# The attention core of a two-layer encoder, unrolled with one more chunk in flight

## The chip, the cores and the metric

The kernel runs on one core of a Trainium2 chip. The metric is the device time of one execution in microseconds (us), as the median over several runs. The core's engines are TensorE (PE; its weight loads are listed as PEld), VectorE (DVE), ScalarE (ACT), GpSimd (POOL) and SyncE (SP, which issues DMAs). Each has its own instruction stream and runs it in order; the streams meet through semaphores alone.

## The reference, cut to what matters

A sequence of 16 meta tokens and 512 tokens, of width 1024, goes through two layers. Each is a half-step SwiGLU FFN, a token mixer and another half-step FFN, all normalised. The mixer of layer 0 is RWKV-7; that of layer 1, which the change concerns, is sliding-window attention with 16 query heads, 4 key/value heads of size 64, a learned sink per head and a relative-position bias. The 512 tokens form 8 chunks of 64; each chunk looks at the 16 meta tokens, the chunk before it and itself.

```python
lc = jnp.einsum('bcqgrd,bckgd->bgrcqk', qc, kb).astype(f32) * scale + bias
lc = jnp.where(valid[:, None, :], lc, NEG_INF)
pc = softmax_with_sink(lc, sink[:, :, None, None, None])
oc = jnp.einsum('bgrcqk,bckgd->bcqgrd', pc.astype(v.dtype), vb).reshape(B, S, G, R, Dh)
o = jnp.concatenate([om, oc], axis=1).reshape(B, L, D)
return o @ w_o + b_o
```

The outputs of the meta queries do not reach the result, so the kernel computes the 8 chunks alone.

## The kernel before

`attention(...)` makes three parts: `start` (projections to queries, keys and values, the bias table), `attend` (the core, lines 2191 to 2395) and `o` (the output projection, through the shared helper whose matmuls are at line 287). All operands of the core are float32, and a float32 matmul shows as two records in the trace.

For a chunk c (slot s = c % 2) the core does the following.

- GpSimd (function `pool`) copies the meta bias (L2238, step `bias`), the queries (L2241, `q`), and for either half of the heads the meta keys (L2250, `km0`, `km1`) and the window's keys (L2252, `kb0`, `kb1`) into slot s, and last the values (L2260, `v`). The bias copy of c waits for the copy `v` of c-1, and the copy `v` of c waits for the values matmuls of c-2 (step `o`), which read the same slot.
- TensorE, scores (L2276): 8 matmuls (16 records of 144 columns; 80 in chunk 0) into PSUM banks 0 to 2 in groups of 3, 3 and 2 pairs of heads (`l0` to `l2`). They wait for `kb1` of c and for DVE's reads of the same bank of c-1.
- DVE, scores (L2353): scale plus bias for each group, from PSUM to `prob`; then the row maximum (L2359), the maximum with the sinks (L2362), its negative (L2365), and the sink's argument (L2367, `ts`).
- ScalarE, exponentials: one for the sinks (L2321) and eight with row sums (L2323, step `p`).
- DVE, normalisation: the sum (L2371), its reciprocal (L2373) and the product over all probabilities (L2376, `p`). This is `softmax`, `normed` in the changed kernel.
- TensorE, turned probabilities: 8 transposes of the window's part (L2289, banks 3 and 4, `tb0`, `tb1`) and 8 of the meta part (L2298, banks 5 and 6, `tm0`, `tm1`).
- The copies of these to SBUF: `tb0` and `tm0` on ScalarE (L2329, L2332), `tb1` and `tm1` on DVE (L2381, L2384). `ptb` and `ptm`, which they write, have one buffer each.
- TensorE, values: 8 pairs of heads, each with a matmul over the window (L2309) and one over the meta tokens (L2310) into bank 7 (32 records, step `o`).
- ScalarE's high half of the result (L2337, `hi`) and DVE's rest (L2389, `lo`), both to `x16` as float16.

The helper `chunks` sets the order on every engine: chunk 0 and 1 are written out, chunks 2 to 7 run in a hardware loop (`Fori`) of two chunks a turn with offsets from a register. Within a step for chunk c, TensorE does scores(c), turned(c-1), values(c-1); DVE does the scores of c, the copies of c-1, the normalisation of c, the rest of c-1; ScalarE the copies of c-1, the exponentials of c, the high half of c-1. `Steps` counts the semaphores; with `lead=2` each starts two chunks ahead, so that waits on chunks -1 and -2 pass. `hold` increments a semaphore of its own between waits on GpSimd.

Of the kernel before, what the change touches and what calls it, by code (L numbers as in the profile page):

```python
# [26 lines left out]
P = 128  # L27
D = 1024
KT = D // P
META = 16  # L30
# [67 lines left out]
def build(nc, xT, vecs, consts, w_gu, w_down, w_rkv, w_l1, w_g1, w_w2, w_a2, w_g2, w_out, w_q, w_k, w_v, b_v,  # L98
          w_o, rel_table, rel_hot, flip_rows, out):
    with ExitStack() as ctx:  # L100
# [1850 lines left out]
        def attention(T, T_out, ffn_before, table_from):  # L1951
# [64 lines left out]
            def bands(e):  # L2016
# [3 lines left out]
                for s in range(2):  # L2020
                    e.dma_start(rev_band[s * CH:(s + 1) * CH],
                                shifted(8 * s * RELS + RELS - WIN, [[RELS, 8], [1, WIN]])).then_inc(s_bias, 16)
                    for ch in range(NCH):
# [16 lines left out]
                            lambda e, k: e.wait_ge(b_dve.sem, b_dve.count("lo", NCH - 1)), (2, 3))  # L2040
# [150 lines left out]
            a_pool = Steps(sem("attn_pool"), ["bias", "q", "km0", "kb0", "km1", "kb1", "v"], lead=2)  # L2191
            a_pe = Steps(sem("scores_pe"), ["l0", "l1", "l2"], lead=2)
            a_dve = Steps(sem("softmax_dve"), ["l0", "l1", "l2", "mx", "mxs", "nm", "ts", "den", "rd", "p"], lead=2)
            a_act = Steps(sem("softmax_act"), ["es", "p"], lead=2)
            b_pe = Steps(sem("values_pe"), ["tb0", "tb1", "tm0", "tm1", "o"], lead=2)
            b_dve = Steps(sem("values_dve"), ["tb1", "tm1", "lo"], lead=2)
            b_act = Steps(sem("values_act"), ["tb0", "tm0", "hi"], lead=2)
# [3 lines left out]
            def chunks(e, *parts):  # L2201


                scores, turned, softmax, values = parts
# [6 lines left out]
                scores(0, 0, CH)  # L2211
                softmax(0, 0, CH)
                step(1, 1)
# [3 lines left out]
                turned(NCH - 1, 1, WIN)  # L2217
                values(NCH - 1, 1, WIN)

            def nothing(*chunk):  # L2220
                pass

            def pool(e):
                a_pool.open(e)
# [6 lines left out]

                def a(c_, s, nb):
                    e.wait_ge(a_dve.sem, a_dve.count("l2", c_ - 2))
                    e.wait_ge(a_pool.sem, a_pool.count("v", c_ - 1))
                    hold(e)
                    e.tensor_copy(bias_t[:, s, :, 0:META],  # L2238
                                  b_meta[:, bass.ds(c_, 1)].rearrange("p o u n -> p (o u) n")).then_inc(
                                      a_pool.sem, a_pool.step("bias"))  # L2240
                    e.tensor_copy(qc[:, s], q_all[:, :, bass.ds(c_ * CH, CH)]).then_inc(a_pool.sem, a_pool.step("q"))  # L2241
                    if nb == CH:
                        band = slice(META, META + CH)
                    else:
                        band = bass.ds(c_ * CH + (META - CH), WIN)
                    for par in range(2):
                        rows = slice(par * HD, (par + 1) * HD)
                        e.wait_ge(a_pool.sem, a_pool.count("kb0" if par else "q", c_))
                        hold(e)
                        e.tensor_copy(kx[rows, 2 * s + par, :, 0:META], kd[rows, :, 0:META]).then_inc(  # L2250
                            a_pool.sem, a_pool.step(f"km{par}"))
                        e.tensor_copy(kx[rows, 2 * s + par, :, META:META + nb], kd[rows, :, band]).then_inc(  # L2252
                            a_pool.sem, a_pool.step(f"kb{par}"))
                    if nb == CH:
                        e.wait_ge(freed, v_at + 1)
                        e.wait_ge(s_vw, 48)
                    e.wait_ge(b_pe.sem, b_pe.count("o", c_ - 2))
                    e.wait_ge(a_pool.sem, a_pool.count("kb1", c_))
                    hold(e)
                    e.tensor_copy(vx[0:nb, s], v_win[0:nb, bass.ds(c_, 1)].rearrange(  # L2260
            "p o n -> p (o n)")).then_inc(a_pool.sem, a_pool.step("v"))
                chunks(e, a, nothing, nothing, nothing)

            def pe(e):
                a_pe.open(e)
                b_pe.open(e)
# [3 lines left out]
                def a(c_, s, nb):  # L2270
                    for z, (u0, u1) in enumerate(groups):
                        e.wait_ge(a_pool.sem, a_pool.count("kb1", c_))
                        e.wait_ge(a_dve.sem, a_dve.count(f"l{z}", c_ - 1))
# [7 lines left out]
                def b(c_, s, nb):  # L2281
                    for h2 in range(2):
                        if h2 == 0:
                            e.wait_ge(a_dve.sem, a_dve.count("p", c_))
                            e.wait_ge(b_act.sem, b_act.count("tb0", c_ - 1))
                        else:
                            e.wait_ge(b_dve.sem, b_dve.count("tb1", c_ - 1))
                        for u in range(4 * h2, 4 * h2 + 4):
                            last = e.transpose(psum[0:nb, 3 + h2, (u % 4) * P:(u % 4 + 1) * P],  # L2289
                                               prob[:, s, u, META:META + nb], c("ident"))  # L2290
                        last.then_inc(b_pe.sem, b_pe.step(f"tb{h2}"))
                    for h2 in range(2):
                        if h2 == 0:
                            e.wait_ge(b_act.sem, b_act.count("tm0", c_ - 1))
                        else:
                            e.wait_ge(b_dve.sem, b_dve.count("tm1", c_ - 1))
                        for u in range(4 * h2, 4 * h2 + 4):
                            last = e.transpose(psum[0:META, 5 + h2, (u % 4) * P:(u % 4 + 1) * P],  # L2298
                                               prob[:, s, u, 0:META], c("ident"))
                        last.then_inc(b_pe.sem, b_pe.step(f"tm{h2}"))  # L2300

                def values(c_, s, nb):
                    e.wait_ge(b_act.sem, b_act.count("tm0", c_))
                    e.wait_ge(b_dve.sem, b_dve.count("tm1", c_))
                    e.wait_ge(a_pool.sem, a_pool.count("v", c_))
                    for u in range(8):
                        g, par = u // 2, u % 2
                        o = psum[par * HD:(par + 1) * HD, 7, g * P:(g + 1) * P]
                        e.matmul(o, vx[0:nb, s, g * HD:(g + 1) * HD], ptb[0:nb, u], start=True, stop=False)  # L2309
                        last = e.matmul(o, v_meta[:, g * HD:(g + 1) * HD], ptm[:, u], start=False, stop=True)  # L2310
                    last.then_inc(b_pe.sem, b_pe.step("o"))
                chunks(e, a, b, nothing, values)

            def act(e):
                a_act.open(e)
                b_act.open(e)
                warm(e, ACT.Exp)

                def a(c_, s, nb):
                    e.wait_ge(a_dve.sem, a_dve.count("ts", c_))  # L2320
# [6 lines left out]
                def b(c_, s, nb):  # L2327
                    e.wait_ge(b_pe.sem, b_pe.count("tb0", c_))
                    e.activation(ptb[0:nb, 0:4], psum[0:nb, 3, :].rearrange("p (u n) -> p u n", n=P),  # L2329
                                 ACT.Copy).then_inc(b_act.sem, b_act.step("tb0"))  # L2330
                    e.wait_ge(b_pe.sem, b_pe.count("tm0", c_))
                    e.activation(ptm[:, 0:4], psum[0:META, 5, :].rearrange("p (u n) -> p u n", n=P),  # L2332
                                 ACT.Copy).then_inc(b_act.sem, b_act.step("tm0"))

                def values(c_, s, nb):
                    e.wait_ge(b_pe.sem, b_pe.count("o", c_))
                    e.activation(x16[:, 0, :, bass.ds(c_ * CH + META, CH)],  # L2337
                                 psum[:, 7, :].rearrange("p (k n) -> p k n", n=CH), ACT.Copy).then_inc(
                                     b_act.sem, b_act.step("hi"))
                chunks(e, nothing, b, a, values)  # L2340

            def dve(e):
                a_dve.open(e)
                b_dve.open(e)
                e.wait_ge(turn_dve.sem, turn_dve.count("read"))

                def a(c_, s, nb):
                    segs = [(0, NKEY, 0)] if nb == WIN else [(0, META, 0), (META, CH, META + CH)]
                    for z, (u0, u1) in enumerate(groups):
                        e.wait_ge(a_pe.sem, a_pe.count(f"l{z}", c_))  # L2350
                        e.wait_ge(a_pool.sem, a_pool.count("bias", c_))
# [6 lines left out]
                    e.wait_ge(a_dve.sem, a_dve.count("l2", c_))  # L2358
                    e.tensor_reduce(mx, prob[:, s, :, 0:META + nb], AX_X, ALU.max).then_inc(  # L2359
                        a_dve.sem, a_dve.step("mx"))  # L2360
                    e.wait_ge(a_dve.sem, a_dve.count("mx", c_))
# [261 lines left out]
```

## Time and profile before

| | us |
|---|---|
| median of three runs | 2396.33 |
| lowest, highest | 2395.67, 2398.77 |
| the profiled execution | 2393.34 |
| its span | 2391.4 |
| the attention core in it (first scores to the output projection) | 1838.97 to 1972.17 |

The profile is of one execution; the times in its rows count from the start of the span, which leaves out about 2 us of the execution. TensorE is busy for 2249.9 us of the span, DVE for 1114.1, ScalarE for 790.8 and GpSimd for 585.5. The granted TensorE clock is told as a share of its full 2.4 GHz; its mean over the span is 0.943. The first matmul records of the core are those of line 2276, and the first record of the part behind it is one of line 287.

### The profile page before, as it was taken

The numbers are of one execution on the slowest core, as the hardware profiler recorded it, in microseconds if no ns is written. First come the engines' busy times: TensorE is split into PE (matmuls) and PEld (weight loads), VectorE is DVE, ScalarE is ACT, GpSimd is POOL, SyncE is SP. The second block draws the span as 40 slices with busy tenths as digits, with TensorE's granted clock in tenths as the row PEclk, the third lists the DMA queues.
The fourth block names the chain that finished last, engine by engine and source line by source line (L and its number), as shares of the span: only waits on it lengthen the run. The fifth ranks groups of instructions, "written<-read, shape, count | busy, mean of one in ns | idle before, by whom it ended". The sixth has DMA issues, their size and how long they took to land.

```text
span 2391.4 us, 51187 instructions
## 1 busy us (share of the span) xinstructions
PE 2249.9 (94%) x22812; PEld 1912.7 (80%) x22812; DVE 1114.1 (47%) x1471; ACT 790.8 (33%) x1347; POOL 585.5 (24%) x676
## 2 busy tenths in 40 slices
PE   7999999789689998999999999999998889999997
PEld 6888887678589984778888888888887557888886
DVE  5434317785655544563342274333274336533423
ACT  4333314751233331353332153333132334433320
POOL 2111114486132210351111151110062104311103
PEclk9999999889699996899999999999998669999998
DMA  4333312220000010223233123233223002323311
GB/s 153 126 105 102 122 60 92 73 72 19 1 3 4 4 38 18 110 91 109 104 109 122 54 71 124 89 115 112 75 62 106 0 0 83 108 93 107 136 59 36
DMA packets 28949, 183.37 MB, mean 77 GB/s; under 512 B 3216, under 2 KB 8144, under 8 KB 9792
## 3 DMA queue, kind: packets, MB, share of 16 engines
q1 hardware_dynamic: 27888, 178.79, 21.4%
q8 instruction: 178, 2.92, 0.5%
q0 software_dynamic: 848, 1.37, 0.3%
q14 instruction: 35, 0.29, 0.0%
HBM read 174.31 MB, written 4.30 MB: 75 GB/s over the span
## 4 chain that ended last, share of the span: by engine, by line
PE 85%; DVE 8%; POOL 3%; ACT 2%; issue 1%; DMA 0%; SPq 0%; POOLq 0%; DVEq 0%; ACTq 0%
PE psum L287 67%; PE psum L1503 6%; POOL h L347 1%; PE psum L2310 1%; PE psum L2309 1%; PE psum L1494 1%; PE psum L311 1%; PE psum L1835 1%; PE psum L1527 1%; PE psum L362 1%; PE psum L2276 1%; PE psum L1837 1%; DVE arena L339 1%; POOL x L398 1%; PE psum L2110 1%
## 5 line engine op out<-in xcount | busy, mean ns | idle before, releaser
L287 PE MATMUL psum<-x,split 128*128 128x256 f16 (+2 forms) x5424 | 621.0, 277 | 9.8 <-POOL x L398 6.3
L287 PEld LDWEIGHTS psum<-x,split 128*128 128x128 f16 (+1 forms) x5424 | 532.7, 98 | 93.4 <-issue 10.5
L287 PE MATMUL psum<-x,split_more 128*128 128x256 f16 (+1 forms) x2688 | 310.5, 277 | 1.5 <-DVE x L2389 1.5
L695 POOL TENSOR_TENSOR arena<-arena 128x256 f16<-128x256 f32 (+1 forms) x176 | 120.1, 682 | 772.3 <-ACT arena L544 772.3
L287 PEld LDWEIGHTS psum<-x,split_more 128*128 128x128 f16 x2688 | 264.8, 99 | 41.3 <-issue 1.9
L287 PE MATMUL psum<-arena,split 128*128 128x256 f16 (+2 forms) x2448 | 279.2, 277 | 4.0 <-ACT arena L1209 4.0
L287 PE MATMUL psum<-x,arena 128*128 128x256 f16 (+1 forms) x2400 | 275.1, 276 | 0.7 <-POOL x L932 0.5
L287 PEld LDWEIGHTS psum<-arena,split 128*128 128x128 f16 (+1 forms) x2448 | 241.2, 99 | 40.5 <-ACT arena L1209 4.7
L262 DVE SCALAR_TENSOR_TENSOR split<-stage,split 128x2048 f16<-128x2048 f32 (+2 forms) x77 | 192.4, 2499 | 161.4 <-ACT split L256 161.4
L287 PEld LDWEIGHTS psum<-x,arena 128*128 128x128 f16 x2400 | 235.1, 98 | 35.4 <-POOL x L932 1.5
L622 DVE SCALAR_TENSOR_TENSOR arena<-psum,arena 128x256 f32<-128x256 f32 (+1 forms) x176 | 75.5, 429 | 320.8 <-ACT arena L538 316.2
L538 ACT ACTIVATE arena<-psum 128x256 f32<-128x256 f32 (+1 forms) x176 | 68.3, 388 | 384.2 <-PE psum L287 384.1
L256 ACT ACTIVATE split<-stage 128x2048 f16<-128x2048 f32 (+2 forms) x77 | 155.3, 2017 | 28.9 <-PE psum L287 27.4
L438 ACT ACTIVATE arena<-arena 128x272 f32<-128x272 f32 (+1 forms) x96 | 38.9, 418 | 360.3 <-DVE arena L425 338.3
L287 PE MATMUL psum<-arena,split_more 128*128 128x256 f16 (+3 forms) x1248 | 144.8, 278 | 11.8 <-POOL arena L961 11.8
L425 DVE TENSOR_SCALAR arena<-psum 128x272 f32<-128x272 f32 (+1 forms) x80 | 33.3, 427 | 249.9 <-PE psum L287 249.9
L287 PEld LDWEIGHTS psum<-arena,split_more 128*128 128x128 f16 (+1 forms) x1248 | 123.3, 99 | 31.2 <-issue 12.2
L449 POOL TENSOR_TENSOR arena<-arena 128x272 f32<-128x272 f32 (+1 forms) x84 | 65.4, 779 | 326.1 <-ACT arena L438 323.0
L544 ACT ACTIVATE arena<-arena 128x256 f16<-128x256 f32 (+1 forms) x176 | 74.0, 421 | 185.9 <-DVE arena L627 185.9
L262 DVE SCALAR_TENSOR_TENSOR split_more<-stage,split_more 128x2048 f16<-128x2048 f32 (+2 forms) x38 | 94.3, 2481 | 83.5 <-ACT split_more L256 83.5
L287 PE MATMUL psum<-arena 128*128 128x256 f16 (+1 forms) x1056 | 120.0, 275 | 0.0
L262 DVE SCALAR_TENSOR_TENSOR arena<-stage,arena 128x2048 f16<-128x2048 f32 (+1 forms) x33 | 84.2, 2550 | 71.0 <-ACT arena L256 71.0
(220 smaller groups left out, 2830.7 us busy)
## 6 DMA issues: line engine op xcount, KB each, us to landing
stage<-in_w_gu SPq DMA_DIRECT2D x88, 1024.0 KB, 4.9
stage<-in_w_down SPq DMA_DIRECT2D x32, 1408.0 KB, 6.1
stage<-in_w_rkv SPq DMA_DIRECT2D x12, 1024.0 KB, 4.9
stage<-in_w_out SPq DMA_DIRECT2D x4, 1024.0 KB, 4.8
stage<-in_w_q SPq DMA_DIRECT2D x4, 1024.0 KB, 4.8
stage<-in_w_o SPq DMA_DIRECT2D x4, 1024.0 KB, 5.7
h_spill<-h SPq DMA_DIRECT2D x1, 2112.0 KB, 8.9
h<-h_spill SPq DMA_DIRECT2D x1, 2112.0 KB, 9.4
```

The source lines that it names most:

```text
L256: act.activation(job.split[:, 0, 0:job.cols], stage[:, job.u, 0:job.cols], ACT.Copy, scale=W_SCALE).then_inc(w_hi, 1)
L262: dve.scalar_tensor_tensor(out=job.split[:, 1, 0:job.cols], in0=stage[:, job.u, 0:job.cols], scalar=W_SCALE, in1=job.split[:, 0, 0:job.col ...
L287: last = pe.matmul(o, wt(wp, k), xs(xp, k), start=(k == 0 and wp == 0 and xp == 0), stop=(k == tiles - 1 and wp == 1))
L311: last = e.matmul(psum[:, b0 + b, 0:m], to, rows[:, a:a + m], start=True, stop=True)
L425: ins = dve.tensor_scalar(mix_out[:, m, a:a + n], bank(i, z)[:, 0:n], 1.0 / W_SCALE, None, ALU.mult)
L438: act.activation(osq[:, q % 2, 0:n], mix_out[:, m, a:a + n], ACT.Square).then_inc(out_sq, 1)
L449: pool.tensor_tensor(ssum[:, a:a + n], ssum[:, a:a + n], osq[:, q % 2, 0:n], ALU.add).then_inc(out_add, 1)
L538: e.activation(gate_s[:, no % 2, 0:n], bank(i)[:, 0:n], ACT.Sigmoid, scale=1.0 / W_SCALE).then_inc(gate_act, 1)
L544: e.activation(hid[s][:, 0, m, 0:n], hid32[:, no % 2, 0:n], ACT.Copy).then_inc(hid_hi, 1)
L622: e.scalar_tensor_tensor(out=gate_x[:, no % 2, 0:n], in0=bank(i)[:, 0:n], scalar=1.0 / W_SCALE ** 2, in1=gate_s[:, no % 2, 0:n], op0=ALU.m ...
L695: e.tensor_tensor(hid[s][:, 1, m, 0:n], hid32[:, no % 2, 0:n], hid[s][:, 0, m, 0:n], ALU.subtract).then_inc(hid_lo, 1)
L1503: last = e.matmul(o[p0:p0 + HD, q], a[p0:p0 + HD, 4 * f + q, 0:CH], b[p0:p0 + HD, 4 * f + q, 0:CH], start=(z == 0), stop=(z == len(terms) ...
```

## The change

The hardware loop and the helper `chunks` are gone, and each engine has its order written out in Python for all 8 chunks, with constant offsets:

| engine | order within the iteration i |
|---|---|
| TensorE | scores(i+1), values(i-1), turned(i) |
| ScalarE | exponentials(i+1), high half(i-1), copies of turned(i) |
| DVE | normalisation(i), scores(i+1), rest(i-1), copies of turned(i) |
| GpSimd | copies of i, as before |

Chunk 0 has its scores and exponentials ahead of the loop, and chunk 7 its values, high half and rest behind it. The semaphores are split into one for each group of steps and start at zero; a wait on a chunk before the first is left out (`after`). Waits added: values(i) for DVE's rest(i-1); DVE's scores(i) for the transposes of i-2 (`tm1`); both engines' copies of i for the values of i-1; GpSimd's query copy of i for the scores of i-2 by TensorE's own semaphore. DVE's wait for the exponentials of the chunk before ahead of L2365 is gone, as is `hold` in the core. The output projection waits for the same event under its new name. The core of the diff:

```diff
-                def step(c_, s):
-                    scores(c_, s, WIN)
-                    turned(c_ - 1, 1 - s, CH if isinstance(c_, int) and c_ == 1 else WIN)
-                    softmax(c_, s, WIN)
-                    values(c_ - 1, 1 - s, CH if isinstance(c_, int) and c_ == 1 else WIN)
-                with e.Fori(0, NCH // 2 - 1) as i:
-                    step(i * 2 + 2, 0)
-                    step(i * 2 + 3, 1)
+            def after(e, steps, name, i):
+                if i >= 0:
+                    e.wait_ge(steps.sem, steps.count(name, i))
...
             def pool(e):
+                for i in range(NCH):
+                    s, nb = i % 2, keys(i)
+                    after(e, a_dve, "l2", i - 2)
+                    after(e, a_pool, "v", i - 1)
+                    e.tensor_copy(bias_t[:, s, :, 0:META], b_meta[:, i]).then_inc(a_pool.sem, a_pool.step("bias"))
+                    after(e, a_pe, "l2", i - 2)
+                    e.tensor_copy(qc[:, s], q_all[:, :, i * CH:(i + 1) * CH]).then_inc(a_pool.sem, a_pool.step("q"))
...
+                    after(e, o_pe, "o", i - 2)
+                    e.wait_ge(a_pool.sem, a_pool.count("kb1", i))
+                    e.tensor_copy(vx[0:nb, s], v_win[0:nb, i]).then_inc(a_pool.sem, a_pool.step("v"))
...
             def pe(e):
+                scores(0)
+                for i in range(NCH):
+                    if i + 1 < NCH:
+                        scores(i + 1)
+                    if i:
+                        values(i - 1)
+                    turned(i)
+                values(NCH - 1)
...
             def act(e):
+                exps(0)
+                for i in range(NCH):
+                    if i + 1 < NCH:
+                        exps(i + 1)
+                    if i:
+                        high(i - 1)
+                    turned(i)
+                high(NCH - 1)
...
             def dve(e):
+                scored(0)
+                for i in range(NCH):
+                    normed(i)
+                    if i + 1 < NCH:
+                        scored(i + 1)
+                    if i:
+                        rest(i - 1)
+                    turned(i)
+                rest(NCH - 1)
```

## Rows read from the trace of the kernel before

**Rows 1.** Windows of the core and behind it: stretch, length, busy by engine, PEclk, DMA.

```profile
1838.97:1972.17 133.20, 114.01 (x513) 76.09 (x514) 55.87 (x107) 41.70 (x161) 20.09 (x50) 0.68 0.02 7
1972.17:2391.40 419.23, 401.17 (x3592) 356.49 (x3592) 174.66 (x206) 131.47 (x198) 95.69 (x124) 0.98 0.25 89
```

**Rows 2.** Windows, scores start to scores start: first and last of five periods.

```profile
1863.48:1879.74 16.26, 13.94 (x66) 9.35 (x65) 7.17 (x13) 5.17 (x20) 2.81 (x7) 0.71 0.01 1
...
1927.56:1943.44 15.88, 13.81 (x65) 9.53 (x64) 7.17 (x13) 5.17 (x20) 2.81 (x7) 0.71 0.00 0
```

**Rows 3.** Windows between changes of the granted clock, the last figure but two.

```profile
1850.40:1867.40 17.00, 14.82 (x54) 8.86 (x52) 6.69 (x13) 4.58 (x19) 2.81 (x7) 0.50 0.00 0
1867.50:1874.20 6.70, 4.38 (x31) 2.76 (x30) 3.97 (x10) 4.58 (x19) 0.00 (x0) 1.00 0.01 2
1874.30:1884.40 10.10, 10.10 (x38) 7.12 (x39) 3.51 (x5) 0.60 (x1) 2.81 (x7) 0.50 0.00 0
...
1939.20:1949.30 10.10, 10.10 (x40) 7.70 (x40) 3.93 (x6) 1.20 (x2) 0.40 (x1) 0.50 0.00 0
...
1952.80:1962.90 10.10, 10.10 (x37) 5.58 (x38) 2.66 (x5) 2.15 (x8) 0.00 (x0) 0.50 0.00 0
1963.00:1969.80 6.80, 5.98 (x37) 3.19 (x34) 1.03 (x2) 0.59 (x1) 0.00 (x0) 1.00 0.01 2
```

**Rows 4.** Waits in the core: waiter, releaser, us in total, times, longest.

```profile
POOL arena L2260 <- PE psum L2310: 80.5, 6, 17.7
...
PE psum L2309 <- DVE arena L2384: 12.2, 6, 2.4
```

**Rows 5.** Order of time in one period: start, us, engine, line, operation.

```profile
1879.74 4.21 PE L2276 MATMUL psum<-arena 128*128 128x144 f32 x16
1880.15 0.40 POOL L2260 COPY arena<-arena 128x256 f32 x1 [12.84 <-PE psum L2310]
...
1882.96 0.61 POOL L2252 COPY arena<-arena 64x512 f32 x1
...
1886.48 0.21 ACT L2321 ACTIVATE arena<-arena 128x8 f32<-128x8 f32 x1 [0.27 <-DVE arena L2367]
...
1887.89 0.43 PE L2309 MATMUL psum<-arena 128*64 128x128 f32 x2 [1.87 <-DVE arena L2384]
...
1889.90 0.17 DVE L2371 TENSOR_TENSOR arena<-arena 128x8 f32<-128x8 f32 x1 [2.24 <-ACT arena L2323]
...
1890.34 1.36 DVE L2376 TENSOR_TENSOR arena<-arena 128x1152 f32<-128x1152 f32 x1
...
1895.30 3.60 PE L2276 MATMUL psum<-arena 128*128 128x144 f32 x16
```

**Rows 6.** Order of time, two turned blocks, of chunks 4 and 7.

```profile
1915.39 1.04 PE L2289 MATMUL psum<-cst,arena 128*128 128x128 f32 x8
...
1916.27 1.04 PE L2298 MATMUL psum<-cst,arena 128*16 128x128 f32 x8
...
1960.65 1.97 PE L2289 MATMUL psum<-cst,arena 128*128 128x128 f32 x8
```

**Rows 7.** Windows with values matmuls alone, of chunks 0 and 7.

```profile
1853.69:1863.48 9.79, 9.79 (x32) 4.50 (x33) 1.73 (x3) 2.14 (x12) 0.00 (x0) 0.50 0.00 0
...
1964.50:1969.80 5.30, 5.25 (x30) 2.83 (x30) 0.00 (x0) 0.00 (x0) 0.00 (x0) 1.00 0.01 3
```

**Rows 8.** Order of time at the start of the core.

```profile
1848.93 1.48 DVE L2353 SCALAR_TENSOR_TENSOR arena<-psum,arena 128x432 f32<-128x432 f32 x3
1849.07 1.06 PE L2289 MATMUL psum<-cst,arena 128*64 128x128 f32 x8 [2.50 <-DVE arena L2376]
...
1852.44 0.21 ACT L2321 ACTIVATE arena<-arena 128x8 f32<-128x8 f32 x1 [1.16 <-DVE arena L2367]
```

**Rows 9.** Order of time, GpSimd's first bias copy and DVE beside it.

```profile
1834.26 2.27 DVE L262 SCALAR_TENSOR_TENSOR split<-stage,split 128x2048 f16<-128x2048 f32 x1
1834.62 2.07 POOL L2238 COPY arena<-arena 128x128 f32<-128x128 f32 x1 [34.15 <-DVE arena L2170]
```

More of the change, by code:

```diff
@@ L2220, in nothing, with keys @@
-            def nothing(*chunk):
-                pass
+            def after(e, steps, name, i):
+                if i >= 0:
+                    e.wait_ge(steps.sem, steps.count(name, i))
+            def keys(i):
+                return CH if i == 0 else WIN
             def pool(e):
-                a_pool.open(e)
                 for par in range(2):
@@ L2253, in a @@
                             a_pool.sem, a_pool.step(f"kb{par}"))
-                    if nb == CH:
+                    if i == 0:
                         e.wait_ge(freed, v_at + 1)
                         e.wait_ge(s_vw, 48)
[L2257 to L2262, printed above, removed]
+                    after(e, o_pe, "o", i - 2)
@@ L2302, in values, with turned @@
[L2302 to L2305, printed above, removed]
+                def turned(i):
+                    s, nb = i % 2, keys(i)
+                    e.wait_ge(n_dve.sem, n_dve.count("p", i))
+                    for name, b0, rows, c0, n in (("tb", 3, nb, META, nb), ("tm", 5, META, 0, META)):
+                        for h2 in range(2):
+                            after(e, t_dve2 if h2 else t_act2, f"{name}{h2}", i - 1)
+                            for u in range(4 * h2, 4 * h2 + 4):
+                                last = e.transpose(psum[0:rows, b0 + h2, (u % 4) * P:(u % 4 + 1) * P],
+                                                   prob[:, s, u, c0:c0 + n], c("ident"))
+                            last.then_inc(t_pe2.sem, t_pe2.step(f"{name}{h2}"))
@@ L2306, in values @@
+                def values(i):
+                    s, nb = i % 2, keys(i)
+                    e.wait_ge(t_act2.sem, t_act2.count("tm0", i))
+                    e.wait_ge(t_dve2.sem, t_dve2.count("tm1", i))
+                    e.wait_ge(a_pool.sem, a_pool.count("v", i))
+                    after(e, o_dve2, "lo", i - 1)
                     for u in range(8):
                         g, par = u // 2, u % 2
-                        o = psum[par * HD:(par + 1) * HD, 7, g * P:(g + 1) * P]
-                        e.matmul(o, vx[0:nb, s, g * HD:(g + 1) * HD], ptb[0:nb, u], start=True, stop=False)
@@ L2310, in values @@
-                        last = e.matmul(o, v_meta[:, g * HD:(g + 1) * HD], ptm[:, u], start=False, stop=True)
-                    last.then_inc(b_pe.sem, b_pe.step("o"))
-                chunks(e, a, b, nothing, values)
+                        o_ = psum[par * HD:(par + 1) * HD, 7, g * P:(g + 1) * P]
+                        e.matmul(o_, vx[0:nb, s, g * HD:(g + 1) * HD], ptb[0:nb, u], start=True, stop=False)
+                        last = e.matmul(o_, v_meta[:, g * HD:(g + 1) * HD], ptm[:, u], start=False, stop=True)
@@ L2314, in act, with exps @@
+                    last.then_inc(o_pe.sem, o_pe.step("o"))
+                scores(0)
[6 more added lines that the diff above has]
+                values(NCH - 1)
             def act(e):
-                a_act.open(e)
-                b_act.open(e)
                 warm(e, ACT.Exp)
-                def a(c_, s, nb):
-                    e.wait_ge(a_dve.sem, a_dve.count("ts", c_))
+                def exps(i):
+                    s, nb = i % 2, keys(i)
+                    e.wait_ge(a_dve.sem, a_dve.count("ts", i))
@@ L2332, in b, with high @@
                     e.activation(ptm[:, 0:4], psum[0:META, 5, :].rearrange("p (u n) -> p u n", n=P),
[L2333 to L2337, printed above, removed]
+                                 ACT.Copy).then_inc(t_act2.sem, t_act2.step("tm0"))
+                def high(i):
+                    e.wait_ge(o_pe.sem, o_pe.count("o", i))
+                    e.activation(x16[:, 0, :, i * CH + META:(i + 1) * CH + META],
@@ L2342, in dve, with scored @@
+                high(NCH - 1)
             def dve(e):
-                a_dve.open(e)
-                b_dve.open(e)
                 e.wait_ge(turn_dve.sem, turn_dve.count("read"))
-                def a(c_, s, nb):
+                def scored(i):
+                    s, nb = i % 2, keys(i)
                     segs = [(0, NKEY, 0)] if nb == WIN else [(0, META, 0), (META, CH, META + CH)]
+                    e.wait_ge(a_pool.sem, a_pool.count("bias", i))
+                    after(e, t_pe2, "tm1", i - 2)
@@ L2375, in softmax, with turned @@
                     pr = prob[:, s, :, 0:META + nb]
                     e.tensor_tensor(pr, pr, rd.unsqueeze(2).to_broadcast([P, 8, META + nb]), ALU.mult).then_inc(
[L2377 to L2380 removed]
+                        n_dve.sem, n_dve.step("p"))
+                def turned(i):
+                    nb = keys(i)
+                    after(e, o_pe, "o", i - 1)
+                    e.wait_ge(t_pe2.sem, t_pe2.count("tb1", i))
```

132 lines of the change are left out of this document (46 added, 86 removed).

## The prediction, made before the result was known

> **What bounds the kernel now.** I read the windows first, then the waits, then the order of time. The attention core runs from 1838.97 to 1972.17 us: 133.2 us, with TensorE busy for 114.0 of them and a granted clock of 0.68 [rows 1]. Behind it lie 419.2 us in which TensorE is busy for 401 at 0.98. Nothing in the change touches that stretch, its weights have a stage of their own, and so what the core gains or loses should reach the end in full. Five loop periods from 1863.48 to 1943.44 take 79.96 us, 15.99 each [rows 2].
>
> A period holds three blocks of TensorE work, on scores, turned probabilities and values. In the period shown, scores start at 1879.74, values at 1887.89, the next scores at 1895.30 [rows 5]. Only one gap is worth having: values wait for copies that DVE makes behind the scores' reductions, 12.2 us in six waits [rows 4]. The rest is TensorE's own time, and that hangs on its clock. The windows show the two levels, 0.50 (1.2 GHz) and 1.00 (2.4 GHz), in long stretches [rows 3]. All values work of chunk 0 ran at 0.50 for 9.79 us with TensorE never idle [rows 7], and the clock did not rise until the scores behind it (1867.5 [rows 3]). It then stayed at 1.00 for 6.7 us, in which TensorE worked 4.4 us only: transposes, the gap, the start of the values. Then it fell within the values. So values do not raise the clock, scores and transposes do, and a good part of what they gain is spent on a gap.
>
> **The three blocks at either level.** Values: 9.8 us low [rows 7]; high, 30 records in 5.30 us at 1.00, so 32 in 5.65 [rows 7]. Scores: 16 records, 4.2 us low [rows 5]; no row shows them all at the high level, so I bound them by half of that, 2.1, and by no gain at all, 4.2, and take 2.1 for a fully high block, as transposes nearly halve: eight take 1.04 us high against 1.97 low, and 0.88 high from start to the next eight's start (1915.39 to 1916.27) [rows 6]. A turned block is two such halves: 1.8 us high, about 3.4 low (0.88 x 1.97 / 1.04, twice).
>
> **What the new order removes.** On TensorE it becomes scores(i+1), values(i-1), turned(i). The copies that values(i-1) wait for belong to a block turned a whole period before. So the gap of 12.2 us goes; its upper bound is all of it, its lower one nothing.
>
> **What is late next.** GpSimd copies values, queries and keys into two slots. Its copy of v(i+1) waits for values(i-1) to be done, and it must come before the keys of i+2. Today that wait is 80.5 us in total and free [rows 4], since scores and turned lie between. In the new order scores(i+2) follow values(i-1) with only turned(i) between. From the end of values at 1879.74 GpSimd starts at 1880.15 and ends its last key copy at 1883.57 (1882.96 + 0.61) [rows 5]; I add 0.25 us for TensorE to start, an estimate below the 0.41 of that first handover. That is 4.1; with constant addresses in place of registers the handovers may be shorter. I take 4.0, in a range of 3.6 to 4.2 as long as nothing blocks GpSimd. Turned(i) fills 1.8 to 3.4 us of it; the rest, 0.6 to 2.2 us, is a new gap, now ahead of the scores.
>
> One steady period is therefore scores + values + 4.0: 2.1 + 5.65 + 4.0 = 11.8 us all high, 4.2 + 9.8 + 4.0 = 18.0 all low, against 15.99.
>
> **Other edits.** DVE's and ScalarE's orders have a ring of their own: normed(i), scored(i+1), exponentials(i+1), normed(i+1). Exponentials take 3.42 us (1886.48 to 1889.90), normed 1.80 (1889.90 to the product's end at 1891.70) [rows 5], scored 3.5 with its three reads back to back (1848.93 to 1852.44 [rows 8]) and up to 1.2 more where low scores pace the reads. Together 8.7 us, at most 9.9, under the 11.8 of TensorE and GpSimd: no cost in the steady part, since those two hide it; uncovered, a period could not be shorter than these 8.7 to 9.9. ScalarE's copies of a turned block stand behind the next exponentials, a delay hidden by the period they now have. The added waits (values on DVE's rest of the chunk before, copies on the values before) name events a block or more old: zero, with DVE's rest of a chunk 0.7 us as the price if one were late. The unrolled streams issue the same instructions with fixed addresses. The loop's turn costs nothing that the five periods show, so I take zero, between 0.4 us gained and 0.4 us lost a period (the handover at 1879.74 again), 3 us in all either way. The final wait of the output projection names the same event. SP's queue is untouched.
>
> **The sum over the core.** Turned(0) starts at 1849.07 as today, nothing before it having changed order. Scores(2) follow it, and values(0) wait for ScalarE's copies, now behind exponentials(1): those start at 1852.44 [rows 8], take 3.42, and two copies follow of 0.6 each: values(0) at 1857.1, 18.1 us after the core's start (today 1853.69). From there: 8 values blocks v, five stretches of 4.0, five scores blocks s (3 to 7), two times turned-to-values at the tail T (chunks 6 and 7, no scores between to hide copies; 1960.65 to 1964.50 today, 3.9 [rows 6, 7]; 2.9 if high), and 2.0 from the last values (1964.5 + 5.7 = 1970.2) to the projection at 1972.17.
> All high: 18.1 + 45.2 + 20 + 10.5 + 5.8 + 2 = 101.6. All low: 18.1 + 78.4 + 20 + 21 + 7.8 + 2 = 147.3. Today 133.2: so from 31.6 gained to 14.1 lost, and the clock decides.
> Where it will be: today a high stretch (6.7 us long in six of eight, 3.3 in two) holds idle time ahead of the values, 2.3 us in the one from 1867.5 [rows 3]. If it opens at the end of the scores, as at 1867.5, it now falls straight on the values and covers most of a block. Today's values blocks average about 8.0 us (7.4 in the period shown, 9.8 in chunk 0, 5.7 in chunk 7); I take v = 7.1, that is 3.6 us of it high, and s = 3.1, halfway, as some high stretches will open in the turned block before, and T = 3.5. These are choices between rows, not readings. Sum: 18.1 + 56.8 + 20 + 15.5 + 7 + 2 = 119.4, a gain of 13.8.
>
> **A rule against this.** The transposes of chunk 7 (from 1960.65 [rows 6]) came after values at 0.50, and by 1963.0 the clock was 1.00 with no scores near [rows 3]: transposes raised it. The Trainium skill, TensorE: Matmul & The Clock Gate, Part 4: PE-mode transpose, says that the full clock does not engage for transposes, as they do not count as busy in the same way; that is rival F, and the trace disagrees with it here.
>
> **Rivals.** A, forecast: high for a good part of the values, 8 to 18 gained. Chance 0.48.
> B, high nearly throughout: without the gap ahead of the values the clock never falls, up to 31.6 gained; say 24, 2369 by this execution. For it: values(7) ran high from 1964.5 to 1969.8 behind turned and a short gap. Against it: seven of today's eight high stretches ended inside values. 0.19.
> C, GpSimd is stretched. Its copy of 128 elements at 1834.62 took 2.07 us, against 0.61 for one of 512 [rows 5], and ended at 1836.7, just after DVE's SBUF-only instruction of 2.27 us did (1836.5) [rows 9]. If DVE's product of normed(i+1), 1.36 us [rows 5], lands on the key copies, each of five stretches is 1.4 longer: 7 back, gain 7. Against it: when everything is high the product starts at about the copies' end, and later when low. 0.15. (The Trainium skill, SBUF — State Buffer, SBUF: two separate sides, has this as an exclusive lock of a port pair between GpSimd and DVE instructions with two SBUF inputs; the trace agrees at this one place.)
> D, the other side: the clock stays low. Values have 9.8 us in which to lose it, the new gap of 0.6 us or more stands right before the scores, and scores behind a gap may be too short to raise it, as those from 1943.44 [rows 2], through which the level stayed at 0.50 up to 1949.3 [rows 3]. Every period is then 18.0 against 15.99, up to 14.1 slower in sum. It decides once v averages above 8.1 with s at 4.2, where the sum reaches today's 133.2. 0.08.
> E, no net gain: v stays at 8.0 with s at 4.2, 7.2 and 5.5 us more than in the sum: 132, about 1 gained. 0.06.
> F, transposes open no high stretch: s stays at 4.2, five times 1.1 more, a gain of 8.3. 0.04.
>
> **Numbers.** The profiled execution takes 2393.34 us with a span of 2391.4; less 13.8 it is 2379.5. The median of the timed runs stands 3.0 us above it, at 2396.33, so the forecast for that median is 2382.6. A alone spans 2378 to 2388; with B and C down to 2368, with the milder part of D and E up to 2396. A measurement of this kernel can tell about 0.2%, 4.8 us, from no change. Faster: A, B, F and most of C, 0.83. Same: a little of C, E, part of D, 0.11. Slower: 0.06.
>
> **What would show it.** Right: gap before values (L2309 of before, DVE's copies as releaser) gone; scores now released by GpSimd's key copies, 4.0 us after the values' end; periods of 13 to 14.5 us; high stretches lying on the values. Wrong: periods near 18 at 0.50 (D); GpSimd copies of over 1 us (C); a gap released by ScalarE or DVE in mid-loop, which would mean that their ring is longer than 9.9.

## The result, and the profile after

The changed kernel takes 2369.39 us in the median of four runs (2368.07 to 2370.23) against 2396.85 for the kernel before: a ratio of 0.9884, interval 0.9867 to 0.9901, 27.5 us less. The forecast was 2382.6 in a range of 2368 to 2396. The time lies in the range, 13.2 us below the forecast and 1.4 above the range's lower end.

The profiled execution took 2368.07 us with a span of 2365.9, 25.5 less than before. The windows of the core and of what is behind it, in the columns of [rows 1]:

```profile
1833.28:1946.87 113.59, 103.28 (x513) 68.39 (x513) 56.50 (x108) 40.82 (x161) 20.38 (x50) 0.73 0.06 21
1946.87:2365.90 419.03, 400.98 (x3592) 356.46 (x3592) 174.57 (x206) 131.49 (x198) 95.83 (x124) 0.98 0.25 89
```

Behind the core nothing changed (419.23 against 419.03). The core is 19.6 us shorter. Of these, TensorE's busy time gives 10.7 (114.01 to 103.28) and its idle time 8.9 (19.19 to 10.31). TensorE's instructions are the same, so less busy time means the same matmuls at a higher clock (0.68 to 0.73 in the mean). Another 5.7 us of the span lie ahead of the core (1838.97 to 1833.28). Most of it is in TensorE's first waits (order of time, the kernel after):

```profile
1833.28 1.98 PE L2253 MATMUL psum<-arena 128*128 128x80 f32 x16 [0.71 <-DVE arena L2170]
1838.16 3.90 PE L2253 MATMUL psum<-arena 128*128 128x144 f32 x16 [2.89 <-DVE arena L2352]
```

The first scores stand 0.71 us behind the last window of the values' projection, against 5.09 before (the idle time in the bracket of the row `1838.97 7.59 PE L2276` of the kernel before). That is 4.4 us. The last 1.3 lie further ahead, in stretches with the same work, and have no cause that a run here shows. The 2.89 us ahead of scores(1) are new, since before scores(0) and (1) ran as one block. The bracket names VectorE, but TensorE's weight load waits for GpSimd's keys of chunk 1, and those stand behind a copy that waits for a DMA (waits):

```profile
POOL arena L2240 <- DMA arena<-arena: 8.5, 1, 8.5
...
PEld psum L2253 <- POOL arena L2233: 3.0, 1, 3.0
```

One period and a half in order of time, in the columns of [rows 5] and from several answers of that view:

```profile
1872.36 3.63 PE L2265 MATMUL psum<-cst,arena 128*128 128x128 f32 x16
1872.50 0.40 POOL L2240 COPY arena<-arena 128x256 f32<-128x256 f32 x1 [9.23 <-PE psum L2279]
1874.96 0.62 POOL L2233 COPY arena<-arena 64x512 f32<-64x512 f32 x1
1875.79 2.16 PE L2253 MATMUL psum<-arena 128*128 128x144 f32 x16
1877.89 0.43 PE L2278 MATMUL psum<-arena 128*64 128x128 f32 x2
1884.34 3.67 PE L2265 MATMUL psum<-cst,arena 128*128 128x128 f32 x16
1887.81 2.96 PE L2253 MATMUL psum<-arena 128*128 128x144 f32 x16
```

L2265 is the turned block (16 records, both kinds), L2253 the scores, L2278 the first of the values. No bracket stands behind a TensorE row: it is never idle here. The turned block of 3.4 us (from its start to that of the scores) ends 0.2 us after GpSimd's chain, which runs from 1872.50 to 1875.58. The period is 12.02 us (1875.79 to 1887.81), against 15.99 before [rows 2]. Windows of three periods, and of the clock's stretches in them (the granted clock is the last figure but two, as in [rows 3]):

```profile
1875.79:1887.81 12.02, 12.02 (x66) 8.03 (x65) 6.93 (x13) 4.94 (x20) 2.83 (x7) 0.78 0.00 0
1887.81:1899.88 12.07, 12.07 (x65) 8.49 (x65) 6.95 (x13) 4.96 (x20) 2.83 (x7) 0.79 0.01 1
1899.88:1911.95 12.07, 12.07 (x66) 8.08 (x65) 6.95 (x13) 5.09 (x21) 2.83 (x7) 0.78 0.00 0
...
1865.90:1872.30 6.40, 6.40 (x39) 3.57 (x37) 3.50 (x8) 2.73 (x14) 0.00 (x0) 1.00 0.00 0
1872.60:1875.70 3.10, 3.10 (x16) 2.44 (x16) 1.38 (x2) 1.95 (x5) 2.73 (x7) 0.50 0.00 0
1876.10:1882.40 6.30, 6.30 (x42) 4.09 (x40) 5.50 (x11) 0.56 (x4) 0.00 (x0) 1.00 0.00 0
1882.80:1889.40 6.60, 6.60 (x29) 5.01 (x28) 2.64 (x6) 3.98 (x16) 2.83 (x7) 0.50 0.00 0
```

In the steady periods a high stretch is as long as before, 6.3 to 6.7 us in such windows, but TensorE works in all of it where it worked 4.4 of 6.7 [rows 3]. It opens in the scores or at the end of the turned block and covers most of the values or all of them, then the clock falls. In the tail the two high stretches are only half as long, 3.1 and 2.8 us.

Not everything is shorter. Values(0) now wait for ScalarE, whose copies stand behind the exponentials of chunk 1:

```profile
1845.84 0.21 ACT L2297 ACTIVATE arena<-arena 128x8 f32<-128x8 f32 x1 [4.72 <-DVE arena L2352]
...
1849.13 0.57 ACT L2307 ACTIVATE arena<-psum 64x512 f32<-64x512 f32 x1
...
1850.23 0.69 PE L2278 MATMUL psum<-arena 64*64 64x128 f32 x2 [3.86 <-ACT arena L2310]
```

### The profile page after: what moved, and what is told of

Read it like the earlier page. It is cut to its first block, busy times and chain, and to the rows that moved or that the text cites. A ratio compares the mean times of both kernels' runs of the same rounds, so it can differ in the third digit from the quotient of the medians.

```text
span 2365.9 us, 50902 instructions
## 1 busy us (share of the span) xinstructions
PE 2236.7 (95%) x22812; PEld 1905.0 (81%) x22812; DVE 1112.4 (47%) x1471; ACT 789.7 (33%) x1347; POOL 584.2 (25%) x676
## 4 chain that ended last, share of the span: by engine, by line
PE 86%; DVE 8%; POOL 3%; ACT 2%; issue 1%; DMA 0%; SPq 0%; POOLq 0%; ACTq 0%; DVEq 0%
PE psum L287 67%; PE psum L1503 6%; POOL h L347 1%; PE psum L362 1%; PE psum L1494 1%; PE psum L311 1%; PE psum L2279 1%; PE psum L2278 1%; PE psum L1835 1%; PE psum L1527 1%; PE psum L2265 1%; POOL x L398 1%; PE psum L1837 1%; DVE arena L339 1%; PE psum L2110 1%
## 5 line engine op out<-in xcount | busy, mean ns | idle before, releaser
L287 PEld LDWEIGHTS psum<-x,split 128*128 128x128 f16 (+1 forms) x5424 | 531.6, 98 | 92.0 <-issue 10.2
```

What stands on the lines that cost most here:

```text
L287: last = pe.matmul(o, wt(wp, k), xs(xp, k), start=(k == 0 and wp == 0 and xp == 0), stop=(k == tiles - 1 and wp == 1))
```

## The experiments

Each run was timed in five rounds beside the kernel before; the ratio is to it. "Core" is the time in the trace from the first scores to the output projection (133.20 before, 113.59 after), "head" the idle time ahead of the first scores (5.09 and 0.71).

**The head alone, on the kernel before.**

```diff
...
             def dve(e):
+                a_dve.open(e)
+                b_dve.open(e)
                 start.vector(e)
...
```

and likewise on the other engines, the old places removed.

> The kernel before with one edit: every engine opens its semaphores of the core before its start part instead of behind it, so GpSimd's copies of chunk 0 need not wait until VectorE has issued the last split. My theory (head): the wait for that opening is what held the first scores 5.1 us behind the last values window, and the changed kernel shows 0.7; so 4 to 5 us faster than before, first scores within 1 us of the last values window, loop periods unchanged at 16 us. Rival (the head's gain comes with the new order or the constants): within 1 us of before.

Ratio 0.9971, interval 0.9962 to 0.9979. Head 0.66, core 132.04. GpSimd's first copy moved from 1834.62 [rows 9] to 1825.49, under the projection of the values:

```profile
1825.49 0.29 POOL L2237 COPY arena<-arena 128x128 f32<-128x128 f32 x1 [25.51 <-issue]
...
1834.07 1.98 PE L2273 MATMUL psum<-arena 128*128 128x80 f32 x16 [0.66 <-issue]
```

The theory of the head holds: 4.4 us of idle time are gone with this one edit. The edit moves the opening on every engine; that VectorE's was the one that counted is shown by the run with the late head below. Scores(0) also run at the high clock now, 1.98 us for 16 records instead of 3.7: in the kernel before the clock had fallen to 0.50 in the gap ahead of them, at 1836.6, and here it is 1.00 up to 1839.7. By the ratio the run is 7.0 us faster (5.0 to 9.1), where 4 to 5 were expected. The trace places 4.4 in the head and 1.2 in the core, and nothing here places the rest.

**Unrolled, in the old order.**

```diff
-                scores(0)
                 for i in range(NCH):
-                    if i + 1 < NCH:
-                        scores(i + 1)
+                    scores(i)
                     if i:
+                        turned(i - 1)
                         values(i - 1)
-                    turned(i)
```

with the orders of ScalarE and VectorE put back to match.

> The changed kernel (unrolled, split semaphores, nothing to open) with the order of before on all engines: scores(c), turned(c-1), values(c-1) and the rest to match. My theory: unrolling by itself gives the head (4.4 us) and perhaps 1 us through shorter handovers, so 5 to 6 us faster than before and 21 to 22 slower than the changed kernel, periods 15.5 to 16 us with a gap of about 2 us before values. Rival (the registers, branches and counted waits cost time in the loop): 10 us or more faster than before.

Ratio 0.9959, 0.9947 to 0.9971, which the head alone reaches within the intervals. That is 9.8 us (7.0 to 12.7), more than the 5 to 6 expected, and the timed runs alone don't exclude the rival's 10. The trace decides: head 0.70, core 132.06, a period of 15.53 of which 1.88 are idle, the gap before the values:

```profile
1833.87:1965.93 132.06, 113.48 (x513) 74.94 (x514) 57.48 (x108) 41.58 (x161) 20.23 (x50) 0.69 0.05 18
1871.95:1887.48 15.53, 13.65 (x65) 9.38 (x64) 7.14 (x13) 5.17 (x20) 2.81 (x7) 0.72 0.00 0
```

The run before this one has the loop, the registers and the early head, and its core is 132.04; so they cost nothing to speak of. What the core gained is the order's: 132.06 against 113.59.

**The new order with the old head.**

```diff
             def pool(e):
...
+                e.wait_ge(dve_here, 1)
                 for i in range(NCH):
...
             def dve(e):
+                e.sem_inc(dve_here, 1)
```

> The changed kernel with GpSimd's first copies made to wait until VectorE has issued its last split, as they did before: the new order without the early head. My theory: 4 to 5 us slower than the changed kernel, hence 22 to 23 faster than before. Rival (the head is later hidden behind the 3.9 us for which values(0) wait for ScalarE): under 1.5 us slower than the changed kernel.

Ratio 0.9912, 0.9899 to 0.9925; about 6.7 us slower than the changed kernel by the ratios, with some 5 us either way by their intervals. Head 4.77, core 113.30. The first copy was again the long one, beside VectorE's last split:

```profile
1836.83 2.57 POOL L2226 COPY arena<-arena 128x128 f32<-128x128 f32 x1 [33.57 <-DVEq L2331]
...
1841.37 3.99 PE L2255 MATMUL psum<-arena 128*128 128x80 f32 x17 [4.77 <-POOL arena L2235]
```

Here GpSimd waits for VectorE alone, and the head is back; so it was VectorE's count, added behind its start work. Head and order add up: 4.1 us of head, the core unchanged. (In this trace the work ahead of the head also ended 4.0 us later than in the changed kernel's, in unchanged work and with no cause shown.)

**ScalarE's first copies ahead of the exponentials of chunk 1.**

```diff
                 exps(0)
+                turned(0)
                 for i in range(NCH):
                     if i + 1 < NCH:
                         exps(i + 1)
                     if i:
                         high(i - 1)
-                    turned(i)
+                        turned(i)
```

> The changed kernel with ScalarE's two copies of turned chunk 0 ahead of the exponentials of chunk 1 instead of behind them; ScalarE is idle there for 4.7 us. Theory: values(0) start at the end of VectorE's copies, 3 us earlier, and fall into the high clock that TensorE still has, so 3 to 6 us faster than the changed kernel. Rival (something else is late in its place: the next exponentials, or the clock's stretches fall elsewhere): within 1 us.

Ratio 0.9871, 0.9856 to 0.9885; core 110.63, 3.0 less. The wait of 3.86 us is one of 0.73, at 1846.93. The intervals of this ratio and the changed kernel's overlap; the trace shows the step, and the timed runs can't tell it.

**A third slot for the values' copies.**

```diff
-                    after(e, o_pe, "o", i - 2)
+                    after(e, o_pe, "o", i - 3)
...
-                    e.tensor_copy(vx[0:nb, s], v_win[0:nb, i])
+                    e.tensor_copy(vx[i % 3][0:nb], v_win[0:nb, i])
```

> The changed kernel with three slots for GpSimd's copies of the values instead of two, so the copy of chunk i+1 waits for the values of i-2 and the key copies of i+2 are early. Theory 1 (TensorE sets the pace: it goes from turned(i) into scores(i+2) without a gap, as the low-clock turned block is as long as GpSimd's chain, both 3.4 us): within 1.5 us of the changed kernel. Rival (the chain of GpSimd is the bound, as I had forecast): 1 to 2 us a chunk faster, 5 to 10 in all.

Ratio 0.9893, 0.9878 to 0.9908; core 113.69 against 113.59, and 3.4 us from the values' end to the scores as before. GpSimd's chain is not the bound: with the copies early, the turned block alone fills that time.

**GpSimd's query copy twice, in chunks 3 to 7.**

> The changed kernel with GpSimd's query copy done twice in chunks 3 to 7, in the chain from the end of the values to the next scores: 0.7 to 0.8 us more a chunk. Theory 1 (chain and turned block end together, no slack): the scores wait that long, 3.5 to 4 us slower in all for five chunks, a little more or less as the clock's stretches move. Rival (there is slack in the chain): within 1 us.

Ratio 0.9914, 0.9900 to 0.9928, 7.2 us slower than the changed kernel by the ratios; by the trace the core is 117.60, 4.0 more, as expected. TensorE now waits for GpSimd ahead of each of the five scores blocks (waits):

```profile
PE psum L2257 <- POOL arena L2237: 1.6, 5, 0.5
```

From turned block to scores it is 3.93 us in each of the five, against 3.43 in the changed kernel: 0.50 of the 0.7 us added. So the chain had about 0.2 us of slack: making it shorter gains nothing, and making it longer costs nearly all that is added. The other 1.5 us lie in other blocks; TensorE's busy time grew by 2.4 in all (105.68 against 103.28), so the clock had a part in them.

**Three slots for values, two for turned probabilities, orders unchanged** (control, on the kernel with the early first copies).

> The kernel with the early first copies, with three slots for the values' copies and two for the turned probabilities, all orders unchanged: a control for the next run. Both theories: within 1.5 us of the kernel with the early first copies if TensorE sets the pace, 5 to 10 us faster if GpSimd's chain does.

Ratio 0.9876, 0.9860 to 0.9891, against 0.9871 with the early first copies alone: no gain.

**Transposes mixed into the values.**

```diff
                     if i:
-                        values(i - 1)
-                    turned(i)
+                        values(i - 1, {2: lambda: turned(i, "tb0"), 3: lambda: turned(i, "tb1"),
+                                       5: lambda: turned(i, "tm0"), 6: lambda: turned(i, "tm1")})
+                    else:
+                        turned(i)
```

(each number is a pair of heads, with the transposes that are issued ahead of it; on ScalarE and VectorE the copies of i come before the high half and rest of i-1).

> As the run before, but the four groups of transposes of chunk i stand between the values matmuls of chunk i-1 instead of behind them, on TensorE; ScalarE and VectorE copy them before the high half and the rest of i-1. Same instructions. Theory (a long run of values matmuls is what loses the high clock): fewer or no falls, periods from 12 down to 10 to 11 us, 6 to 14 us faster than its control, mean clock of the core above 0.80. Rival (the clock falls all the same, and the values of i now wait for the high half of i-1): within 2 us of the control or up to 8 slower.

Ratio 0.9905, 0.9890 to 0.9921, core 117.10: 7 us slower than its control, as the rival had it; the 6 to 14 us faster of the theory did not come. Yet the windows of its clock show both sides:

```profile
1853.60:1867.00 13.40, 13.40 (x50) 7.95 (x50) 6.22 (x12) 4.94 (x20) 2.97 (x6) 0.50 0.01 1
1867.40:1890.90 23.50, 22.74 (x144) 14.20 (x142) 15.21 (x28) 9.77 (x40) 7.10 (x15) 1.00 0.00 1
1891.40:1904.40 13.00, 13.00 (x49) 7.90 (x48) 5.97 (x12) 4.94 (x20) 3.17 (x6) 0.50 0.00 0
1904.90:1925.00 20.10, 18.20 (x113) 10.79 (x112) 11.71 (x24) 9.77 (x40) 0.55 (x2) 1.00 0.01 1
```

These high stretches are 23.5 and 20.1 us, three times those of the changed kernel (the longest in the kernel with the early first copies is 10.1, from 1841.6). That speaks for the theory that the long run of values had ended them, but does not show it alone, since ScalarE and VectorE changed their order as well. And the low ones are 13 us, some 10 of them mixture (1853.6 to scores at 1863.6, 1891.4 to scores at 1900.8): in it the clock stays at 0.50, and it rises 3.5 to 3.8 us into the scores behind it. The falls came beside short waits of TensorE, of 2.6 us for chunk 1's probabilities, 0.3 and 0.5 at 1888.2 and 1890.1, and 2.0 at the tail.

**The same with those waits worked on.** Chunk 1 unmixed; ScalarE's high half ahead of its copies; the last values in PSUM bank 0.

```diff
+                    if i == 1:
+                        values(0)
+                        turned(1)
-                    if i:
+                    elif i:
                         values(i - 1, {2: ...
```

> The kernel with the transposes mixed into the values, with its three stalls worked on: chunk 1 unmixed (its transposes waited 2.6 us for VectorE and the clock fell), ScalarE's high half ahead of the copies (values and transposes of chunk 4 and 5 waited 0.3 and 0.5 us and the clock fell again), and the last values into a free bank so as not to wait for VectorE's rest. Theory (a mixed stream keeps a high clock as long as nothing stalls it, and can't raise a low one): once high, all later periods near 10.2 us with no fall before the tail; 10 to 20 us faster than the mixed kernel, 2353 to 2363 us. Rival (the long high stretch was chance): still 2370 or more.

Ratio 0.9839, 0.9826 to 0.9853, core 103.49. One high stretch of 54 us, with periods of 10.2 us in it (scores at 1869.16, 1879.36, 1889.54, 1899.73):

```profile
1859.30:1913.70 54.40, 52.09 (x327) 32.26 (x325) 38.79 (x71) 24.89 (x102) 11.91 (x22) 1.00 0.00 1
1869.16:1879.36 10.20, 10.20 (x66) 6.44 (x65) 7.30 (x13) 4.85 (x21) 3.84 (x7) 1.00 0.01 2
1914.00:1940.90 26.90, 23.77 (x86) 11.84 (x85) 4.07 (x5) 6.77 (x8) 0.00 (x0) 0.50 0.00 1
```

It ended 2.1 us behind a wait of 1.6 us ahead of values(6). That the waits alone ended the stretches is not shown: chunk 1 changed its order as well, and this stretch went on through waits of 0.50 us at 1860.9 and 0.18 at 1862.6, about as long as the two beside the fall at 1891.0 in the first mixed kernel. It was not chance: the next two versions of this kernel have the same stretch, 54 us (plain tail) and 51 us (values copied later).

**The last values into a free bank, alone** (on the kernel with the early first copies).

> The kernel with the early first copies, and the last values into a PSUM bank that is free by then: values(7) no longer wait for VectorE's rest of chunk 6, but for their own copies only. Theory: the gap ahead of the last values is set by the copies of their own transposes as much as by the rest, so within 1 us of the kernel with the early first copies. Rival: 1 us or more faster.

Ratio 0.9870, 0.9855 to 0.9885, against 0.9871: nothing, as expected; the wait ahead of values(7) stays 0.8 us.

**A plain tail: chunk 7's transposes behind the values of chunk 6.**

```diff
-                    if i == 1:
-                        values(0)
-                        turned(1)
+                    if i in (1, NCH - 1):
+                        values(i - 1)
+                        turned(i)
```

> The tuned mixed kernel with the transposes of chunk 7 behind the values of chunk 6 instead of among them. In the mixed tail the clock fell at the stall ahead of values(6) and then stayed low for the mixture and all of the last values (24.0 us from values(6) to the end of values(7); the unmixed tail of the kernel with the early first copies took 22.2). Theory: a low mixture can't raise the clock, a dense turned block may: 1 to 4 us faster. Rival (values at the low clock take their 9.8 us in either order): within 1 us.

Ratio 0.9826, 0.9813 to 0.9840, median 2354.66 us: the lowest of the study, 43 us under the kernel before timed beside it. The interval overlaps that of the run before, but the core's 3.6 us less are what was expected. Its core is

```profile
1833.66:1933.57 99.91, 91.10 (x512) 58.35 (x513) 57.28 (x108) 39.87 (x161) 23.37 (x50) 0.87 0.07 24
1911.58:1932.10 20.52, 19.67 (x80) 10.34 (x80) 3.36 (x5) 1.78 (x3) 0.00 (x0) 0.64 0.00 1
```

and the tail, in the second row, 20.5 us instead of 24.0.

**Values copied behind the next chunk's keys.** GpSimd's copy of values(0) waits for a DMA, and scores(1) wait behind it.

> As the run before, and GpSimd copies the values of a chunk behind the keys of the next one, so the scores of chunk 1 no longer stand 2.9 us behind those of chunk 0 for a copy that waits for a DMA. Theory: scores(1) move up by 2.9 us, but turned(0) stays bound by the chain over VectorE and ScalarE, so 0 to 1 us faster. Rival (scores(0) and (1) back to back change where the clock's first stretches fall): 2 us or more either way.

Ratio 0.9835, 0.9819 to 0.9850: not faster, and the timed runs can't tell it from the run before. Scores(0) and (1) ran as one block of 4.67 us, but turned(0) then came 4.5 us later. The clock fell by the end of that gap: the turned block took 3.55 us instead of 1.94, and the core 101.92 instead of 99.91.

## Why the prediction was right, and where it was off

The sum's terms as they were put, and as the trace of the kernel after has them, block start to block start:

| term | forecast | measured |
|---|---|---|
| core's start to values(0) | 18.1 | 16.95 |
| 8 values blocks | 8 x 7.1 = 56.8 | 8 x 7.04 = 56.3 |
| 5 stretches, values' end to scores | 5 x 4.0 = 20 | 5 x 3.43 = 17.2 |
| 5 scores blocks | 5 x 3.1 = 15.5 | 5 x 2.59 = 12.9 |
| 2 turned-to-values at the tail | 7.0 | 8.7 |
| last values to the projection | 2.0 | 1.5 |
| core | 119.4 | 113.6 |

- **"Turned(0) starts at 1849.07 as today, nothing before it having changed order"** failed, and it is the step that cost most: turned(0) started at 1842.47. The order had not changed, but the diff let all semaphores start at zero, and with that took away VectorE's opening count, which stood behind its whole start part. The prediction has no term for this; it was put at nothing without a reason, though the change was listed. The run with the early opening and the one with the late head each put 4.1 to 4.4 us on it. In the sum it would have made 2378.2.
- **The gap before the values** went as forecast, in the middle of the core. Ahead of chunk 0 the wait for ScalarE is what the sum had in it (forecast 1857.1 less 1838.97; measured 1850.23 less 1833.28); the run with the first copies ahead shows that the order of one pair of copies avoids it.
- **GpSimd's chain** was mis-sized. I took 4.0 us in a range of 3.6 to 4.2; from the values' end to the scores it is 3.43. The chain starts 0.14 us behind the values instead of 0.41, and its last copy ends 3.2 us behind their end instead of 3.8. So the new gap of 0.6 to 2.2 us never came, and the sign that I named for being right, scores released by GpSimd's key copies, did not show. The third slot shows that the chain costs nothing now, the doubled copy that it was 0.2 us from doing so. That holds for turned blocks at the low clock; behind one at the high clock (1.8 us) the chain would be the bound again, an estimate from these rows that no run tests. The periods of 12.0 us lie below the 13 to 14.5 that I had named.
- **The clock** was right in mechanism. High stretches fall on the values, whose mean of 7.04 us is close to the forecast's 7.1, a choice between rows and so in part luck. Scores came out at 2.59 instead of 3.1 us, as in two of five periods the clock was up by the first 0.1 us of them. The turned blocks paid for it, nearly all low; at the tail that is the 8.7 against 7.0.
- **Rivals.** A, the forecast, missed its own numbers: the core gained 19.6 us where A had 8 to 18, and the median lies below A's span of 2378 to 2388, in the part of the range that was there for B and C. For A that is luck: 4.4 us of the gain were not foreseen, and even without them the time, 2373.8, would lie below A's span. B had the nearest number (2369 for its execution, 2368.07 measured), but not its reason: it wanted a clock that never falls, and the clock falls in every period. The time came from A's mechanism, the head, and smaller sizes. C's stretched copies did not occur in the changed kernel's core (GpSimd's copies of 64x64 take 0.23 us each, VectorE's product 1.358 in the mean of seven); they did in the mixed one, where the two met:

```profile
1877.29 1.77 DVE L2369 TENSOR_TENSOR arena<-arena 128x1152 f32<-128x1152 f32 x1
1877.90 1.25 POOL L2231 COPY arena<-arena 64x64 f32<-64x64 f32 x1
```

  against 1.36 and 0.23 us in the changed kernel. (The Trainium skill, SBUF — State Buffer, SBUF: two separate sides, has an exclusive lock between the two for such a pair; the trace agrees.) D and E fell with the periods of 12. F fell in the tail. The clock had fallen at 1920.2, at the end of values(5), and it rose within the turned block of chunk 6, with no scores since 1914.8 (and once more at 1937.2, between the turned block of chunk 7 and the last values, behind values that ran low):

```profile
1920.67 3.39 PE L2265 MATMUL psum<-cst,arena 128*128 128x128 f32 x16
...
1923.50:1923.75 0.25, 0.25 (x3) 0.20 (x2) 0.00 (x0) 0.22 (x1) 0.00 (x0) 0.71 0.00 0
1923.75:1924.00 0.25, 0.25 (x3) 0.03 (x1) 0.00 (x0) 0.25 (x1) 0.00 (x0) 1.00 0.00 0
```

  (The Trainium skill, TensorE: Matmul & The Clock Gate, Part 4: PE-mode transpose, says that the full clock doesn't engage for transposes; here too the trace disagrees.)

The forecast was 13.2 us too slow. Of these, 5.8 are the core (119.4 against 113.6), 4.4 the head, 1.3 the unchanged work ahead of it, and 1.7 come from the step from execution to median, which was 3.0 us before and 1.3 after. The median moved 27.5 us by the runs and the span 25.5 by the profiled executions, 1.5 of it in stretches with unchanged work.

## What to carry to other kernels

Read a diff for the semaphore counts that it removes as well as for the order: a count added behind an engine's earlier work is a wait on that work. When a gap is closed beside a clock that rises and falls, ask where the high stretch falls afterwards; here more of the core's gain was the clock's (10.7 us of TensorE's busy time) than that of idle time (8.9). And work of one kind in whose blocks the clock falls may keep it when it is mixed with other work, as in three runs here for 51 to 54 us, provided that something else has raised the clock first. How long a stall it bears is open: 0.50 us did not end the stretch, and it ended behind 1.6.

## What the runs showed of the hardware that was not expected

The same TensorE instructions in two orders ran at the high level for 6.3 to 6.7 us at a time in the steady periods (values as one block of 32 records), and for 54 us (at most 8 values records in a row between transposes or scores). The mixture that kept a high level for five periods did not regain it: in the first mixed kernel 10.0 and 9.4 us of it, TensorE never idle, passed at 0.50 until scores followed.
